# Weight sums of the last product's seven-product form: from VectorE to adding transfers between memory tensors

## The reference

```
h = rms_norm(x, norm_ffn)
gate, up = split(h @ w_gate_up, 2)            # 1024 -> 2 x 2816
x = x + (silu(gate) * up) @ w_down            # 2816 -> 1024
```

## Time and profile before

| | before |
|---|---|
| median of 3 runs | 1349.94 us |
| the profiled execution | 1350.07 us |
| its span | 1348.3 us |
| PE busy | 1330.7 us (99%) |
| DVE busy | 849.5 us (63%) |
| ACT busy | 632.7 us (47%) |
| POOL busy | 53.9 us (4%) |
| read from memory, written | 112.18 MB, 4.19 MB |

### The profile page before, as it was taken

How to read it: one execution, slowest core, us unless ns; L and a number is a source line. 1 busy time by engine, 2 the same in 40 slices (tenths; PEclk the granted TensorE clock), 3 DMA queues, 4 the chain that set the end, 5 groups by cost and what they waited for, 6 DMA issues and landing times. The chain is left out here.

```text
span 1348.3 us, 17806 instructions
## 1 busy us (share of the span) xinstructions
PE 1330.7 (99%) x6813; PEld 1097.3 (81%) x6813; DVE 849.5 (63%) x1351; ACT 632.7 (47%) x1179; POOL 53.9 (4%) x38
## 2 busy tenths in 40 slices
PE   9999999999999999999999999999999999999998
PEld 7888878887777788888788887888898888888886
DVE  5786654358888744344558876767454565656668
ACT  6554433358888643224426466663343332333333
POOL 0026300000000000000010000000000000000000
PEclk9999999999999999999999999999999999999999
DMA  4222213243111164222261200102425312431321
GB/s 170 82 80 90 63 63 109 94 120 93 39 63 49 51 229 146 99 91 66 93 191 60 72 17 17 32 1 78 142 78 187 126 42 83 140 112 63 107 81 63
DMA packets 33621, 120.66 MB, mean 89 GB/s; under 512 B 3716, under 2 KB 5124, under 8 KB 32258
## 3 DMA queue, kind: packets, MB, share of 16 engines
q1 hardware_dynamic: 32962, 118.48, 26.3%
q10 hardware_dynamic: 576, 1.05, 0.4%
HBM read 112.18 MB, written 4.19 MB: 86 GB/s over the span
## 5 line engine op out<-in xcount | busy, mean ns | idle before, releaser
L1029 PE MATMUL bank<-a_hi,whi 128*128 128x512 f32 (+1 forms) x880 | 346.8, 394 | 0.5 <-DVE a_lo L2467 0.5
L1029 PE MATMUL bank<-a_hi,wlo 128*128 128x512 f32 (+1 forms) x880 | 336.9, 383 | 0.0
L1029 PE MATMUL bank<-a_lo,whi 128*128 128x512 f32 (+1 forms) x880 | 335.9, 382 | 0.0
L1484 ACT ACTIVATE whi<-wraw 128x1024 fp32r<-128x1024 f32 x170 | 176.2, 1055 | 197.0 <-PE bank L1029 126.2
L1884 DVE TENSOR_TENSOR wlo<-wraw,whi 128x1024 fp32r<-128x1024 f32 x170 | 206.8, 1232 | 66.2 <-ACT whi L1484 62.9
L1029 PEld LDWEIGHTS bank<-a_hi,wlo 128*128 128x128 f32 x880 | 165.4, 188 | 32.9
L1029 PEld LDWEIGHTS bank<-a_hi,whi 128*128 128x128 f32 x880 | 166.1, 189 | 31.5 <-issue 2.3
L1029 PEld LDWEIGHTS bank<-a_lo,whi 128*128 128x128 f32 x880 | 165.8, 188 | 31.1 <-issue 1.7
L1029 PE MATMUL bank<-arena 128*128 128x128 f32 (+6 forms) x1012 | 138.8, 287 | 3.0 <-DVE arena L2106 1.2
L1029 PEld LDWEIGHTS bank<-arena 128*128 128x128 f32 (+1 forms) x1012 | 123.2, 189 | 12.8 <-issue 5.3
L1029 PE MATMUL bank<-whi,a_hi 128*128 128x512 f32 x288 | 114.9, 399 | 1.5 <-DVE wlo L1884 0.7
(11 more groups left out here) (273 smaller groups left out, 1939.0 us busy)
## 6 DMA issues: line engine op xcount, KB each, us to landing
wraw<-in_wblk SPq DMA_DIRECT2D x170, 512.0 KB, 3.9
arena<-in_quarters SPq DMA_DIRECT2D x8, 1024.0 KB, 8.6
arena<-in_quarters SPq DMA_DIRECT2D x4, 768.0 KB, 6.6
arena<-in_x SPq DMA_DIRECT2D x4, 512.0 KB, 6.2
arena<-in_x SPq DMA_DIRECT2D x1, 2048.0 KB, 8.5
spill<-arena SPq DMA_DIRECT2D x4, 512.0 KB, 7.3
arena<-spill SPq DMA_DIRECT2D x1, 2048.0 KB, 9.4
out<-arena SPq DMA_DIRECT2D x8, 256.0 KB, 2.0
```

The costliest lines, as they stand in the source:

```text
L1029: return nc.tensor.matmul(o, lhsT, rhs, start=start, stop=stop, **kw)
L1484: A(whi[n % 2][:, cols], wraw[i][:, 0:cols.stop - cols.start], ACT.Copy).then_inc(s_hi, 1)
```

## The change

The twelve `tsum` steps go. Their work is done by 48 memory-to-memory transfers on POOL's queue, into a new tensor `sums`: for each group and each half (piece) of the quarters, a chain of eight transfers, four copies and four that add onto what is there. The six chains run two at a time, in two lanes with a semaphore each; each transfer waits for the one before in its lane. They are hung on every third gemm step from block 22 on, and wait there for DVE's first piece of that block (`s_lo`), so they end at block 39. [...]

All 106 blocks are now loaded by the same loop, the products' from `quarters` or `sums`. From block FF0 = 63 on there are four slots for pieces (the two of `wraw` and two in `arena` at 32 KB), so that a piece may be loaded once DVE has finished the block two before. A product's load of a sum also waits for its chain.

```diff
-SUMS = ("t1", "t2", "t3", "t4")
+SUMS = ("t1", "t3", "t2", "t4")
+SUMMING = (("t1", "b11", False), ("t3", "b12", False), ("t1", "b12", True), ("t3", "b22", True), ("t2", "t1", False),
+           ("t2", "b22", True), ("t4", "t2", False), ("t4", "b21", True))
+SUBTRACTED = {(6, (0, 1)), (7, (1, 1))}
...
+FF0 = block_of("ff_gate")
+SUM_CHAINS = [(group, i) for group, (a, e) in enumerate(FFP) for i in range(2)]
+SUM_LANES = 2
+SUM_EVERY = 3
+SUM_JOBS = [(chain, k) for first in range(0, len(SUM_CHAINS), SUM_LANES) for k in range(len(SUMMING))
+            for chain in range(first, min(first + SUM_LANES, len(SUM_CHAINS)))]
+SUM_STEPS = [s for s in STEPS if s[0] == "gemm" and s[1] >= block_of("gate")][::SUM_EVERY]
+SUM_AT = dict(zip(SUM_STEPS, SUM_JOBS))
+def sums_before(chain, k):
+    return sum(c % SUM_LANES == chain % SUM_LANES for c, _ in SUM_JOBS[:SUM_JOBS.index((chain, k))])
...
+        def raw_of(n, i):
+            slot = i if n < FF0 else (2 * (n - FF0) + i) % 4
+            count = n + 1 if n < FF0 else (n - FF0) // 2 + 1 + (FF0 if slot < 2 else 0)
+            cols = piece(n, i)
+            at = wraw[slot] if slot < 2 else late_raw[:, slot - 2, :]
+            return at[:, 0:cols.stop - cols.start], s_w[slot], 16 * count
...
-            for at, n in enumerate(LOADED):
-                for group, name in QUARTERS_AT.get(n, ()):
...
-                    sp.dma_start(raw[name][:, cols], src[:, cols]).then_inc(s_raw[name], 16)
+            for n in range(NB):
                 for i in range(2):
-                    if n >= 1:
-                        sp.wait_ge(s_lo, 2 * LOADED[at - 1] + i + 1)
-                    cols = piece(n, i)
-                    sp.dma_start(wraw[i][:, 0:cols.stop - cols.start], dram["wblk"][at][:, cols]).then_inc(s_w[i], 16)
+                    before = n - (1 if n <= FF0 else 2)
+                    if n == FF0 + 1:
+                        sp.wait_ge(s_split, max(SPLITS.index(x) for x in SPLITS if x[:2] == ("turn", "hgrn")) + 1)
+                    elif before >= 0:
+                        sp.wait_ge(s_lo, 2 * before + i + 1)
+                    if BLOCKS[n]["form"] == "product" and PRODUCTS_OF[BLOCKS[n]["product"]][1] in SUMS:
+                        chain = SUM_CHAINS.index((BLOCKS[n]["group"], i))
+                        sp.wait_ge(s_presum[chain % SUM_LANES], 16 * sums_before(chain, len(SUMMING) - 1) + 16)
+                    tile, landed, _ = raw_of(n, i)
+                    sp.dma_start(tile, weights_of(n, i)).then_inc(landed, 16)
...
-            def tsum(group, i):
...
-                v.tensor_tensor(r[out_], r[left], r[right], ALU.subtract).then_inc(s_tsum, 1)
...
+            def sum_weights(step):
+                chain, k = SUM_AT[step]
+                (group, i), (name, addend, onto) = SUM_CHAINS[chain], SUMMING[k]
+                n = PRODUCT_AT[group, 1]
+                src = sums[4 * group + SUMS.index(addend)] if addend in SUMS else dram["quarters"][4 * group + QUARTERS.index(addend)]
+                dst, cols = sums[4 * group + SUMS.index(name)][:, piece(n, i)], piece(n, i)
+                pool.wait_ge(s_lo, 2 * step[1] + 1)
+                if sums_before(chain, k):
+                    pool.wait_ge(s_presum[chain % SUM_LANES], 16 * sums_before(chain, k))
+                if onto:
+                    pool.dma_start(dst, src[:, cols], accum_op=ALU.add).then_inc(s_presum[chain % SUM_LANES], 16)
+                else:
+                    pool.dma_start(dst, src[:, cols]).then_inc(s_presum[chain % SUM_LANES], 16)
...
             for s in STEPS:
+                if s in SUM_AT:
+                    sum_weights(s)
```

More of the change, by code:

```diff
@@ L297, in plan @@
             f = ff(c, a, whole)
-            sums = [("tsum", group, 0)] if c == e - 2 else []
-            steps += f[:2] + untaken + sum([H(x) + S(x) for x in unsplit], []) + f[2:4] + sums + f[4:]
+            steps += f[:2] + untaken + sum([H(x) + S(x) for x in unsplit], []) + f[2:]
             untaken, unsplit = [], [c]
-        steps[-2:-2] = [("tsum", group, 1)] + ([] if woven else S(e - 1)[:1])
+        steps[-2:-2] = [] if woven else S(e - 1)[:1]
         made = products(group, (e - a) // 2)
@@ L306, in plan @@
                 untaken, unsplit = H(*unsplit), []
-            sums = {6: [("tsum", group, 2)], 7: [("tsum", group, 3)]}.get(p, [])
             added, rounded = [S(e - 1)[i:i + 1] if p == i and not woven else [] for i in (1, 2)]
             if rounded:
-                steps += m[:1] + untaken + rounded + m[1:-1] + sums + m[-1:]
+                steps += m[:1] + untaken + rounded + m[1:]
             else:
-                steps += m[:2] + untaken + m[2:5] + added + m[5:-1] + sums + m[-1:]
+                steps += m[:2] + untaken + m[2:5] + added + m[5:]
             untaken = [("take", m[0][1])]
@@ L591 @@
 LOADED = [n for n, b in enumerate(BLOCKS) if b["form"] != "product"]
[L592 to L597, removed]
 PRODUCT_AT = {(b["group"], b["product"]): n for n, b in enumerate(BLOCKS) if b["form"] == "product"}
@@ L613, in end_of, with emit @@
     return max(ends)
+FF0 = block_of("ff_gate")
[8 more added lines that the diff above has]
+    return sum(c % SUM_LANES == chain % SUM_LANES for c, _ in SUM_JOBS[:SUM_JOBS.index((chain, k))])
 T_READY = [sum(s[0] == "tile" for s in PRODUCTS[:p + 1]) for p in range(len(PRODUCTS))]
-def emit(nc, dram, spill, out):
+def emit(nc, dram, spill, sums, out):
     ctx = ExitStack()
@@ L778, in emit @@
         hsq = mem(4, [512])
-        raw = {name: mem(kb, [BLK]) for name, kb in (("b11", 0), ("b12", 8), ("b21", 16), ("b22", 24), ("t1", 32))}
-        raw.update(t2=raw["b11"], t3=raw["b12"], t4=raw["b21"])
+        late_raw = mem(32, [2, PIECE])
         half_chunk = T // 2
@@ L816, in emit @@
         assert used[0] <= CMASK0
-        s_w = [sem(f"s_w{i}") for i in range(2)]
+        s_w = [sem(f"s_w{i}") for i in range(4)]
         s_sw = sem("s_small_weights")
@@ L865, in emit @@
         s_kcl = sem("s_kc_rest")
-        s_raw = {name: sem("s_quarter_" + name) for name in QUARTERS}
-        s_tsum = sem("s_weights_summed")
+        s_presum = [sem(f"s_weight_sums{i}") for i in range(SUM_LANES)]
         s_h, s_hsum, s_hround = sem("s_hidden_made"), sem("s_hidden_summed"), sem("s_hidden_rounded")
@@ L954, in _, with weights_of @@
             sp.dma_start(swraw[:, 0:NK * SH], dram["w_dt"]).then_inc(s_sw, 16)
-            for at, n in enumerate(LOADED):
-                for group, name in QUARTERS_AT.get(n, ()):
[L957 to L965, removed]
-                    sp.dma_start(raw[name][:, cols], src[:, cols]).then_inc(s_raw[name], 16)
-                for i in range(2):
-                    if n >= 1:
-                        sp.wait_ge(s_lo, 2 * LOADED[at - 1] + i + 1)
-                    cols = piece(n, i)
-                    sp.dma_start(wraw[i][:, 0:cols.stop - cols.start], dram["wblk"][at][:, cols]).then_inc(s_w[i], 16)
+            def weights_of(n, i):
+                cols = piece(n, i)
+                if BLOCKS[n]["form"] != "product":
+                    return dram["wblk"][LOADED.index(n)][:, cols]
+                group, name = BLOCKS[n]["group"], PRODUCTS_OF[BLOCKS[n]["product"]][1]
+                if name in QUARTERS:
+                    return dram["quarters"][4 * group + QUARTERS.index(name)][:, cols]
+                return sums[4 * group + SUMS.index(name)][:, cols]
@@ L1474, in round_weights @@
                 cols = piece(n, i)
[L1475 to L1484, removed]
+                tile, landed, count = raw_of(n, i)
+                act.wait_ge(landed, count)
+                A(whi[n % 2][:, cols], tile, ACT.Copy).then_inc(s_hi, 1)
             def round_small(kind):
@@ L1879, in rest_of_weights @@
                 cols = piece(n, i)
[L1880 to L1885, removed]
+                v.tensor_tensor(wlo[n % 2][:, cols], raw_of(n, i)[0], f32(whi[n % 2][:, cols]), ALU.subtract).then_inc(s_lo, 1)
             def rest_of_small(kind):
@@ L2030, in hadd @@
                 dve.wait_ge(s_h, c + 1)
-                link(v.tensor_tensor(hsum[:, 0, :], a21, a22, ALU.add))
+                link(v.tensor_tensor(hsum[:, 0, :], a21, a22, ALU.subtract))
                 link(v.tensor_tensor(hsum[:, 1, :], hsum[:, 0, :], a11, ALU.subtract))
-                v.tensor_tensor(hsum[:, 3, :], a12, hsum[:, 1, :], ALU.subtract).then_inc(s_hsum, 1)
-            def tsum(group, i):
[L2037 to L2050, removed]
-                v.tensor_tensor(r[out_], r[left], r[right], ALU.subtract).then_inc(s_tsum, 1)
+                v.tensor_tensor(hsum[:, 3, :], a12, hsum[:, 1, :], ALU.add).then_inc(s_hsum, 1)
             def take(n):
@@ L2061, in take @@
                         x = x2[:, 2 * rows_half + t, 512 * cols_half:512 * cols_half + 512]
-                        last = v.tensor_tensor(x, x, bank[BANK[g]][:, :], ALU.subtract if b["product"] == 4 else ALU.add)
+                        last = v.tensor_tensor(x, x, bank[BANK[g]][:, :],
```

(6 more changed lines are left out.)

## The result

The changed kernel takes 1353.67 us, median of 12 runs (1352.5 to 1354.5), the kernel before in the same series 1349.98 (1349.29 to 1350.65): ratio 1.0027, 95% interval 1.0018 to 1.0036. It is slower by 3.7 us. The profiled execution takes 1353.26, its span is 1351.4: 3.1 us over the one before. It is one of the quicker of the twelve: four executions took 1354.3 us and more with a granted clock of 0.998 or 0.999 (one more at 1354.4 had 1.0), and no trace of such a one is kept.

A forecast was written before the change was run, and what follows sets the result against it. PE was taken as the bound. Profiled 1350.07 - 0.34 (sums) + 0 (loads) + 1.1 (transfers) + 0 (descriptors) = 1350.8; the median, 0.13 below the profiled execution, gives 1350.7 us, range 1349.2 to 1354.5.

The forecast's parts named there:

- What bounds the kernel: PE, busy 99% of the span; removing the sums from DVE can give back at most 1.12 us.
- Part 1: Sums leave DVE: the hole at the last product closes, -0.34 us, between 0 and -1.12.
- the hole before P6: PE's wait at 1323 us, before the last group's third product; no removed instruction lies there, so it stays.
- Part 2: The products' weights come as blocks, loaded a block further ahead: cost 0, up to +1 if a landing is long.
- Part 3, the place: Block 32's weights, queued behind in_x at about 470 us, delayed by block 31's three POOL transfers.
- Part 3, the size: Block 32's landing slips 3.75 us, an add priced as a copy, against 2.65 us of slack: +1.1 us.
- The rule for the add: An add reads two sources, halving its rate; by that rule block 32's stall would be 2.35 us, not 1.1.
- Elsewhere the slack is several us, so it isn't met again: Outside block 32 the transfers cause no stall; block 33's slack is 6.7 us.
- The descriptors: POOL's descriptor work slowing DVE in blocks 22 to 29: taken 0, upper end +20 us.
- Rival (a): Block 32 lands within its slack, so only the -0.34 us remains: 1349.6 us; chance 0.17.
- (b): Transfers hold the engines much longer than a same-size load, at block 32's weights, 482 to 490 us: 1354.5; chance 0.19.
- (c): Lanes so slow that POOL is late for the second layer's attention; decides above 17.8 us per transfer; chance 0.03.

The follow-up runs named there:

- e1: Changed kernel without its 48 transfers and SP's waits for them, products loading a quarter in place of each sum; 1349.69 us, ratio 0.9997 to the kernel before.
- e3: Changed kernel with block 31's three jobs passed over, all later jobs moved on by three places; 1349.98 us, ratio 0.9998 to the kernel before.
- e2: Kernel before, keeping its sums on DVE, plus the 48 transfers into a tensor nobody reads; 1353.66 us, ratio 1.0025 to the kernel before.
- e4: Changed kernel with its 24 adding transfers made plain copies of the same bytes; 1351.77 us, ratio 1.0013 to the kernel before.
- e5: Changed kernel with the jobs begun at block 24 and block 31's passed over; 1350.43 us, ratio 1.0002 to the kernel before.
- e7: Changed kernel with the jobs begun at block 54, in the second layer's attention; 1350.45 us, ratio 1.0002 to the kernel before.

## Why the prediction was right in part

The measured time lies in the range, by the mechanism of part 3, not at the forecast: 1350.7 was forecast, with 0.74 for no change, and the time is 3.0 us above it. That it stayed within the range is in part luck: the upper end, 1354.5, was worked out from prices (1.5 copies for a copy, 3 for an add) that the runs don't show.

- **What bounds the kernel**: right. 24 us of DVE went away and PE's 300 us without a hole stayed. All that this side gave is 0.3 us.
- **Part 1**: right in place and size. The last matmul comes 0.33 us earlier than the delay at block 104 would have it, the span ends 0.31 earlier, against 0.34, and the hole before P6 is left. A step on the way was off without consequence: the takes moved up by 1.1 us (1336.97 to 1339.32 less 3.46), not by 0.6.
- **Part 2**: right, 0, and e1 shows it alone.
- **Part 3, the place**: right. The three jobs of block 31, behind `in_x`, are the loss; e3 removes it by moving them.
- **Part 3, the size**: this is the step that failed. The term was 3.75 - 2.65 = +1.1 and measured 2.33 in the profiled execution, 3.6 in e2's, and some 3.7 by the medians of the changed kernel and e3. Both numbers in it were off. The slip of the landing was 4.6 us (e2: 5.2), not 3.75. "I take the add at a copy's price": in engine time it is 2.07 times that. And a copy was taken at the 420 GB/s of the slices, 1.25 us, where it costs 1.50: `in_x`, which has two copies beside it, lands 3.0 us later. By these prices the three jobs hold the engines 1.5 + 1.5 + 3.1 = 6.1 us, of which 4.6 showed at the second piece; where the rest went stays open, and three copies alone (e4) made it slip 4.2. The slack was 2.3 us, not 2.65, and 4.6 - 2.3 is the hole. In e2 and e4 PE also stood at the first piece, to which the sum gave no term.
- **The rule for the add**: the Trainium skill (page "Collectives: The Full Stack", the section on the bandwidth ceiling) has two source reads halve the rate, there for rings between cores. The ratio 2.07 agrees with it. That the sum by that rule, 2.35, is the profiled execution's 2.33 is luck: it kept the 1.25 and the 2.65, and e2's execution has 3.6.
- **Elsewhere the slack is several us, so it isn't met again**: wrong at 313 us, where the transfer in need was no weight load; in e5 (block 34) and e7 (block 60) two more such places showed themselves.
- **The descriptors**: 0, right: a `wlo` piece of 290 to 470 us takes 1.20 us before and after, and e3 and e7 lose nothing by them. The page "SBUF — State Buffer" of the Trainium skill (section "SBUF: two separate sides") would have it so for two-input forms.
- **Rival (a)** fell by e2 and the result. **(b)** came true in its kind and its place: the three jobs hold the engines for 4.9 of the 1.25 us that the prediction gave a copy, against the 4.5 from which (b) was to decide, and the time passed its bound of 2.7 us. But the slip that it asked for, 5.7 us, was not reached (4.6 and 5.2), and "much longer than a load of its size" holds for the add alone. **(c)** is far off: in pairs a copy lands after 6.4 us and an add after 7.9 (medians; the longest 12.2), against 17.8.

The chance of slower, 0.22, looks too low in hindsight: the term was priced by the cheap end of a row that the trace did not have, at the one place where the slack was known to be short.

## What to carry to other kernels

Work taken off an engine that nobody waits for is worth the holes it closes, here 0.3 of 25 us, and a transfer that replaces it is free only where the DMA engines have slack. Look not at the mean share of DMA (0.20 to 0.40 in this stretch before) but at the bursts, at every consumer behind them in the same queue, and at a job's release time: jobs hung on the semaphore that releases the loads set out together with them each time, and where a burst is queued already that is dear. If such transfers must be made, try one at a time: here that took the loss away.

## What the runs showed of the hardware

- An adding memory-to-memory transfer of 4 KB rows costs the DMA engines 2.07 times a copy (1093 and 529 engine-us for 11.5 MB each, changed kernel and e4). A copy between memory tensors moves 349 GB/s of engine time, loads by the same measure 367 (470 to 482 us before).
- POOL spends 0.53 us on the issue of a copy and 0.83 us on that of an add. Beside them DVE's `wlo` pieces take what they took (1.20 us, 290 to 470 us).
- Two queues are served side by side, and a small transfer needn't wait for a big one issued just before on the other: the copy of 471.40 us landed at 479.9, `in_x` of 471.32 at 482.8. With two copies and then an add under way the pieces behind 2.5 MB landed 2.4 and 4.6 us later than before, with one copy at a time 1.0 and 1.2.
